# Two memory key tiles multiplied at the block border instead of in the first attention of block 2

## What is computed

```
memn = layer_norm_2(mem, ln_mem_g, ln_mem_b)          # once
def memory_cross_attn(x, memn, wq, wkv, wo):          # in each of the two layers of block 2
    q = x @ wq
    k, v = jnp.split(memn @ wkv, 2, axis=-1)          # does not depend on x
    ...
# border of the blocks
x = first_block(...)                                  # ends with layer_norm(x + ffn)
x = layer_norm_2(x, ln_in_g, ln_in_b)                 # second_block begins
h = x @ w_in[0]
```

## Time and profile before

| | us |
|---|---|
| median of 3 runs | 1728.51 |
| lowest and highest of them | 1723.71, 1728.75 |
| the profiled execution, its own time | 1727.46 |
| its span in the profile | 1725.7 |
| PE busy | 1577.0 (91%) |
| DVE busy | 1080.4 (63%) |
| ACT busy | 743.3 (43%) |

### The profile page before, as it was taken

How to read it: one execution, slowest core, us unless ns; L and a number is a source line. 1 busy time by engine, 2 the same in 40 slices (tenths; PEclk the granted TensorE clock), 3 DMA queues, 4 the chain that set the end, 5 groups by cost and what they waited for, 6 DMA issues and landing times.

```text
span 1725.7 us, 27579 instructions
## 1 busy us (share of the span) xinstructions
PE 1577.0 (91%) x11573; PEld 1491.7 (86%) x11573; DVE 1080.4 (63%) x1690; ACT 743.3 (43%) x1056; POOL 62.7 (4%) x58
## 2 busy tenths in 40 slices
PE   6889899999888999977989889999889899899996
PEld 6889899998788999967978888999889788889996
DVE  6975955556866864565444637767754546476766
ACT  4554433333463433332555344445435553344442
POOL 0200000000100000000000000000000000000000
PEclk8989999998899999997979999999988899999999
DMA  9423555554333565552522624655535146255551
GB/s 309 150 79 106 183 188 180 194 178 154 110 101 117 196 219 181 186 195 81 165 79 89 219 78 158 205 196 178 188 95 180 49 138 195 88 181 177 190 190 55
DMA packets 215423, 267.47 MB, mean 155 GB/s; under 512 B 7382, under 2 KB 196740, under 8 KB 215172
## 3 DMA queue, kind: packets, MB, share of 16 engines
q1 hardware_dynamic: 210404, 260.48, 46.1%
q10 hardware_dynamic: 4896, 5.25, 0.9%
HBM read 260.46 MB, written 5.24 MB: 154 GB/s over the span
## 4 chain that ended last, share of the span: by engine, by line
PE 76%; DVE 12%; DVEq 3%; ACT 3%; issue 2%; POOL 2%; DMA 0%; SPq 0%; POOLq 0%; ACTq 0%
PE psw L591 17%; PE psw L592 17%; PE psw L593 17%; PE psa L591 6%; PE psa L592 5%; PE psa L593 5%; DVE wlo L1336 3%; PE psa L727 2%; POOL rstd L1926 2%; PE psw L710 1%; PE psw L954 1%; DVE sy L1410 1%; DVE xtok L1365 1%; PE psw L1043 1%; PE psw L1025 1%
## 5 line engine op out<-in xcount | busy, mean ns | idle before, releaser
L1336 DVE TENSOR_TENSOR wlo<-raw,whi 128x2048 fp32r<-128x2048 f32 x226 | 511.1, 2265 | 328.0 <-ACT whi L1062 327.5
L1062 ACT ACTIVATE whi<-raw 128x2048 fp32r<-128x2048 f32 x226 | 427.0, 1889 | 364.0 <-PE psw L593 261.1
L591 PE MATMUL psw<-xhi,whi 128*128 128x256 f32 x1536 | 436.8, 284 | 2.6 <-ACT r L1195 1.4
L592 PE MATMUL psw<-xlo,whi 128*128 128x256 f32 x1536 | 436.1, 284 | 0.0
L593 PE MATMUL psw<-xhi,wlo 128*128 128x256 f32 x1536 | 435.8, 284 | 0.0
L591 PEld LDWEIGHTS psw<-xhi,whi 128*128 128x128 f32 x1536 | 296.3, 193 | 5.8 <-issue 2.8
L592 PEld LDWEIGHTS psw<-xlo,whi 128*128 128x128 f32 x1536 | 296.4, 193 | 1.2
L591 PE MATMUL psw<-whi,xhi 128*128 128x256 f32 (+2 forms) x992 | 289.4, 292 | 8.2 <-DVE xlo L1377 8.2
L593 PEld LDWEIGHTS psw<-xhi,wlo 128*128 128x128 f32 x1536 | 296.3, 193 | 0.0
L592 PE MATMUL psw<-wlo,xhi 128*128 128x256 f32 (+2 forms) x992 | 287.2, 290 | 0.0
L593 PE MATMUL psw<-whi,xlo 128*128 128x256 f32 (+2 forms) x992 | 286.8, 289 | 0.0
(11 more groups left out here) (249 smaller groups left out, 1964.6 us busy)
## 6 DMA issues: line engine op xcount, KB each, us to landing
raw<-in_w_gu SPq DMA_DIRECT2D x44, 1024.0 KB, 5.1
raw<-in_ffn_w_up SPq DMA_DIRECT2D x44, 1024.0 KB, 5.1
raw<-in_w_in SPq DMA_DIRECT2D x26, 1024.0 KB, 5.3
raw<-in_w_down SPq DMA_DIRECT2D x22, 1024.0 KB, 4.9
raw<-in_ffn_w_down SPq DMA_DIRECT2D x22, 1024.0 KB, 4.8
raw<-in_xa_wkv SPq DMA_DIRECT2D x16, 1024.0 KB, 5.4
raw<-in_w_o SPq DMA_DIRECT2D x8, 1024.0 KB, 5.0
raw<-in_w_pg SPq DMA_DIRECT2D x8, 1024.0 KB, 5.0
```

The costliest lines, as they stand in the source:

```text
L591: pe.matmul(o, lh, rh, start=first, stop=False)
L592: pe.matmul(o, lh, rl, start=False, stop=False)
L1062: nc.scalar.activation(tile_flat(whi, NW, i), tile_flat(raw, NL, i), ACT.Copy).then_inc(hi_ready, 1)
L1336: v.tensor_tensor(tile_flat(wlo, NL, i), tile_flat(raw, NL, i), tile_flat(whi, NW, i).bitcast(F32), ALU.subtract).then_inc(lo_ready, 1)
```

## The change

Tiles 0 and 1 of the memory keys of layer 1 of block 2 (`AT_BORDER`) leave the first attention stage of block 2 and stand in the order of tiles directly behind block 1's last tile. PE multiplies them there in four halves, each into a PSUM bank of its own (`psw`, banks 0 to 3), before `norm_turns`; ACT stores them there. The first attention stage of block 2 keeps four halves, in steps 2, 6, 10 and 12; steps 0, 4, 8 and 11 lose theirs. DVE's `serve` behind block 1's last tile moves to between the two token tiles of the norm, and two serves for the moved tiles follow behind the norm.

```diff
+SLOTS2_FIRST = (2, 6, 10, 12)
...
-    return [(block - 1, 4 * l + k) for k in range(4)]
+    return [(block - 1, 4 * l + k) for k in range(4)][2 if (block, l) == (2, 0) else 0:]
+AT_BORDER = [(1, 0), (1, 1)]
...
+    for lm, k in AT_BORDER:
+        tiles.append(((2, "kv", lm, k), rows(w["xa_wkv_2"][lm])[:, :, k * TC:(k + 1) * TC]))
...
     def memory_slot(block, l, step):
+        if (block, l) == (2, 0):
+            return 20 + SLOTS2_FIRST.index(step) if step in SLOTS2_FIRST else None
...
-                if n:
+                if n and not 16 < n < 20:
                     pe.wait_ge(kv_staged, n)
...
+            for n in range(16, 20):
+                memory_half(n, psw[:, n - 16, :])
+            pe.wait_ge(kv_staged, 20)
             norm_turns((2, "in", 0), psw)
...
+            for n in range(16, 20):
+                memory_store(n, stage[0][:, n % 2, :], psw[:, n - 16, :])
+                if n % 2:
+                    serve((2, "kv", 1, n // 2 % 8))
             for stored_half in kv_stored:
-                act.wait_ge(stored_half, 16 * 8)
+                act.wait_ge(stored_half, 16 * 10)
...
                     if next_key is not None:
                         norm(next_key, xtok, 2, lambda t: (dve.drain(), half_stats(xtok, t)), [t])
+                        if t == 0:
+                            serve(key)
...
-            serve((1, "d", L - 1, FS - 1))
+            serve((2, "kv", 1, 0))
+            serve((2, "kv", 1, 1))
```

More of the change, by code:

```diff
@@ L672, in p_turns, with memory_half @@
                 ins.then_inc(p_turned, 1)
-            def memory_half(n):
+            def memory_half(n, bank):
                 key, half = (2, "kv", n // 16, n // 2 % 8), n % 2
@@ L686, in memory_half @@
                     if key[3] < 4:
-                        ins = product(psa[:, 3, 0:TC], wh[:, k, piece], wl[:, k, piece], memhi[:, k, :],
+                        ins = product(bank[:, 0:TC], wh[:, k, piece], wl[:, k, piece], memhi[:, k, :],
                                       memlo[:, k, :], k == 0, k == KD - 1)
                     else:
-                        ins = product(psa[:, 3, 0:TC], memhi[:, k, piece], memlo[:, k, piece], wh[:, k, :],
+                        ins = product(bank[:, 0:TC], memhi[:, k, piece], memlo[:, k, piece], wh[:, k, :],
                                       wl[:, k, :], k == 0, k == KD - 1)
@@ L714, in attention @@
                     if n is not None:
-                        memory_half(n)
+                        memory_half(n, psa[:, 3, :])
                     if i - 2 >= first:
@@ L1079, in p_high, with memory_store @@
                 nc.scalar.activation(pT_hi, bank2(psw, bank), ACT.Copy).then_inc(p_hi, 1)
-            def memory_store(n, place):
+            def memory_store(n, place, bank):
                 if n % 2:
@@ L1088, in memory_store @@
                     act.wait_ge(kv_stored[n % 2], 16 * (n // 2))
-                nc.scalar.activation(place, psa[:, 3, 0:TC], ACT.Copy).then_inc(kv_staged, 1)
+                nc.scalar.activation(place, bank[:, 0:TC], ACT.Copy).then_inc(kv_staged, 1)
                 act.wait_ge(kv_staged, n + 1)
@@ L1114, in attention @@
                     if half is not None:
-                        memory_store(half, stage[block - 1][:, half % 2, :])
+                        memory_store(half, stage[block - 1][:, half % 2, :], psa[:, 3, :])
                     if i - 1 >= first:
```

## The result

The change made the kernel slower. The median went from 1727.92 us (6 runs of the kernel before, 1723.71 to 1728.75) to 1734.04 us (6 runs, 1732.32 to 1734.49); the ratio is 1.0038 with a 95% interval from 1.0026 to 1.0050, which is 4.5 to 8.6 us. The forecast was 1727.1, its range 1721.5 to 1733.0: the result lies outside.

The account below looks back on a forecast made before the run. PE was taken to carry 76% of the chain that ended last, DVE 12%, with the border DVE's and the attention PE's. Border +4.4 and attention -5.8 made -1.4 us, so 1727.1 from the median 1728.51; range 1721.5 to 1733.0.

Parts of the forecast that it names:

- Border, PE: nothing: Between blocks 1 and 2, the four moved halves fit PE's idle time, with 4.8 us of cover; no cost.
- Border, ACT and its DMAs: nothing: Between blocks 1 and 2, four stores and two more splits fit into ACT's idle time; no cost.
- Border, DVE: +4.4: Two more splits of 2.2 us ahead of `xlo` delay block 2's first product by 4.4 us, to about 795.3.
- Border, clock: 0: Before block 2's first product the clock falls again, with the same slow start behind it; no gain or loss.
- the clock holds over the border: Rival: halves keep PE working in the gap, the next product runs at full clock; -3.6 us, 1724.9, chance 0.10.
- Attention: -5.8: Block 2's first attention stage gains 5.8 us from losing the halves of steps 0, 4, 8 and 11.
- Step 0: First attention of block 2: without the half, PE's transposes start earlier; gain 0.8 us.
- Steps 11 and 12: First attention of block 2: `pv` no longer stands behind a half, the next waits for copies; gain 2.3 us.
- PEclk 1.00 throughout: Sign in block 2's first attention: PE's granted clock stays full while the stage takes 59.8 us.
- The clock falls in the attention: Rival: without halves, one stretch of some 14 us drops to 0.50; +7.2 us in sum, 1735.7, chance 0.06.
- PE bounds the attention wholly: Rival: all 11.2 us of PE work taken from the attention come back; -6.8 us in sum, 1721.7, chance 0.07.
- the halves were fully hidden: Rival: the attention gives back only steps 0 and 4, 1.3 us; +3.1 us in sum, 1731.6, chance 0.07.

Follow-up runs that it names:

- e2: Changed kernel with DVE's border splits reordered: one split before `xlo` as before the change, two behind it; 1729.50 us, ratio 1.0011 to the kernel before.
- e7: Changed kernel with 9 useless matmuls in each of steps 4 and 8 of the attention; attention 61.92 us, 1725.23 us in one run.
- e4: Changed kernel with its four remaining halves in steps 0, 4, 8 and 12 instead of 2, 6, 10 and 12; 1727.41 us, ratio 0.9987.
- e12: e5 unchanged, profiled a second time; attention 60.78 us with 4.3 at 0.50, 1720.09 us in one run.
- after: The changed kernel itself, in its first profile; attention 66.38 us with 17.5 at 0.50, median 1734.04 us, ratio 1.0038.
- e3: Kernel before with the four moved halves left out altogether, none at the border either; attention 72.96 us, 1734.79 us, ratio 1.0031.
- e10: Changed kernel, unchanged, profiled a second time; attention 66.36 us with 17.5 at 0.50, 1733.40 us in one run.
- e11: Changed kernel, unchanged, profiled a third time; attention 66.39 us with 17.5 at 0.50, 1733.09 us in one run.
- e5: Changed kernel with both the border order of e2 and the steps of e4; 1722.72 us, ratio 0.9976; its profiled attention 65.91 us with 15.5 at 0.50.
- e8: Changed kernel with the border order of e2 and 24 useless matmuls in each of steps 4 and 8; attention 61.99 us, 1724.82 us, ratio 0.9977.
- e6: Changed kernel with 24 useless matmuls in step 4 alone; attention 63.65 us, 1728.87 us in one run.
- e1: Changed kernel with 24 useless matmuls in each of steps 4 and 8 of the attention; attention 62.39 us, 1728.07 us, ratio 1.0001.

## Why the prediction was wrong

Step by step, in its own order.

- **Border, PE: nothing.** Right. The halves began 0.23 us behind the last matmul of block 1, where I had 0.4, and ended 4.86 us before the turns where DVE's order is the old one (e2); the cover had been put at 4.8.
- **Border, ACT and its DMAs: nothing.** Right: `xhi` was made as soon as the turns were, and e2, which keeps all stores, has the old border.
- **Border, DVE: +4.4.** Right: 29.31 - 24.90 = 4.41, and e2 takes all of it back. The place of the first product, 795.3, was not met (791.41), and nor was the range of 793 to 798 named for it, because this execution had reached the border 3.9 us earlier. I should have given it from PE's last matmul, not from the start of the span.
- **Border, clock: 0.** Right: the clock is at 0.50 from 778.5, when the halves have been over for 4.8 us, until 795.4, and the stage behind it took 92.10 us for 91.94. Filling the first half of the gap moved the fall and not the slow start. The rival "the clock holds over the border" fell with this. This also agrees with what the forecast cited from the Trainium skill (TensorE: Matmul & The Clock Gate, "HAM oscillation — how this bites in real kernels"), that behind a wait between bursts the next burst starts slow.
- **Attention: -5.8.** This is the step that failed; it came to +0.72. The terms were right at the clock for which they were worked out. Step 0: the transposes started 4.22 us behind the scores where it had been 5.02, the 0.8 forecast. Steps 11 and 12: from the half of step 10 to the end of the stage 17.72 us for 19.90, 2.2 us where 2.3 was forecast. Steps 4 to 12 together gave 5.03 of 5.0 in e7. What was named as a sign, no wait before `pv` in step 5, was seen (907.58 follows on 906.42), but because PE was slow and not because the copies were early. The whole stage took 60.6 and 60.8 us in e4 and e12, with 4 us at 0.50, against a forecast of 59.8 without any. What failed is the clause "PEclk 1.00 throughout", the clock's cost in the attention, which the sum had at nothing: PE was at half clock for 17.5 us, nearly all of them busy. By an estimate from these windows, the same work at full clock takes some 8.8 us less, and 66.38 - 59.8 = 6.6 of it reached the end of the stage; that the waits took in the rest is inferred. So the 0.8 us of step 0 was lost again at once, in transposes of 1.11 us and scores of 2.08.
- **The rivals.** "The clock falls in the attention", at 0.06, is what happened. Its size was near partly by luck: it let one stretch of 14 us fall, in steps 3 to 6 or 7 to 10, and got +8.6 for it; here two falls of 7 us and one of 3.5 cost 6.6, and the 3.5 came behind step 0, which it had not named. As a sum, +7.2 forecast by that rival stands against the measured +6.1, and 1735.7 against 1734.04. "PE bounds the attention wholly" and "the halves were fully hidden" are out by e7, e4 and e12: with the clock up, 5 us of the 11.2 come back, neither all nor the 1.3 of steps 0 and 4.
- **The range.** It was said to leave out what lies beyond -6 and +5 us, but 1721.5 to 1733.0 is -6.0 and +5.5 from the profiled execution and -7.0 and +4.5 from the median. The result lies outside by any of these.

**What misled me.** I took one stretch at 1.00, from 139.40 to 149.10 with PE busy for 6.85 us of 9.70, as evidence that pieces of this kind keep the clock, and gave the warning against it 0.06. Ahead of the fall at 901.0 PE was busy for 4.79 us of the 7.00, much the same share:

```profile
894.00:901.00 7.00, 4.79 (x43) 3.89 (x42) 4.30 (x22) 4.56 (x17) 0.00 (x0) 1.00 0.06 21
```

So the busy share of a stretch could not exclude a fall. The timeline of the stretch that I had leaned on, in the kernel before, shows what the share hides:

```profile
139.58 2.00 PE L727 MATMUL psa<-r,pt 128*128 128x64 f32 x16 [0.17 <-ACT pt L1124]
...
143.20 2.00 PE L727 MATMUL psa<-r,pt 128*128 128x64 f32 x16 [0.74 <-ACT pt L1124]
...
146.26 1.97 PE L648 MATMUL psw<-ident,r 128*128 128x128 f32 x16 [1.06 <-DVE r L1653]
```

Its idle comes in pieces of at most 1.06 us; ahead of the fall at 901.0 it is 2.32 in one piece, and PE was busy for 1.29 us of the last 3.50. That is a difference of the two stretches and no rule: e12 held the clock behind 1.79 us. I worked out that `pv` of step 4 would start only 0.5 us earlier than before. I did not write down what the same numbers say, that PE would be idle for 2.8 - 0.5 = 2.3 us there, which is just the wait measured, nor that it would be idle for 2.8 - 0.8 = 2.0 us in step 0, where 2.05 was measured. The section "A second HAM failure mode: psum-queue depth-cycling" of the same page of the Trainium skill tells of a kernel in which small idles between groups of matmuls made the clock swing; rows of after, e3, e10 and e11 agree with it in this stage (0.50 behind waits of 1.84 to 2.32 us), while those of e12 show a wait of 1.79 us without a fall.

**What is shown and what is open.** Shown: the border's 4.4 us are the two splits that were added ahead of `xlo` (e2). The attention's loss is the clock: more time at 0.50 went with a longer stage in after, e2 and e3 (17.5, 22.1 and 31.9 us with 66.4, 68.0 and 73.0) and in two executions of one kernel (e12 and e5), and matmuls that compute nothing shortened it (e8 against e2, e6 against after; e1 and e7 with the reservation above). The changed kernel repeats it (e10, e11). Open: why e4 and e12 mostly keep the clock with the same amount of work, and why the fall ends when it does. Their halves stand in every fourth step from 0, which is a matter of where the lumps of idle are and of when, but no run varied that alone: e4 and e5 also move a store on ACT and a split on DVE. That the waits bring the falls on is argued from what precedes them and from the fills, not shown for each: a wait of 1.79 us had a fall behind it in e5 and none in e4 and e12, and the wait of 1.84 us in step 8 had one in after and none in e6 for the next 6 us. Nor is it known how often e5_both falls; two profiles of it show two outcomes, and why executions enter the stage differently is open too. That the pieces of attention are narrow matmuls (64 to 256 columns) was not separated from their being thin in time. And whether any of the 3.4 us by which the rest differed (780.6 in all profiles of after, 777.2 and 780.8 in those of before) is the change's cannot be told from two profiles of before.

## What to carry to other kernels

Work that PE does "in a wait" may be what keeps the clock of TensorE up: before taking it away, list the idle that each removal uncovers, and price the work behind it at the half clock as well as at the full one. If filler has to move, leave what remains at the places with the longest waits (here steps 0, 4 and 8) rather than spread by convenience: e4 changed three numbers, and its ratio is 0.9987 where that of the changed kernel is 1.0038. It is no cure, since moving the halves opens other waits: in e4 and e12 the longest is now 3.74 us, in step 7, with the one fall behind it. And work moved into another engine's chain goes behind the operation that the next stage waits for: two splits moved behind `xlo` were worth 4.4 us, and both edits together made the version that beats the two kernels, 0.9976 (0.9959 to 0.9993) of the time before.

## What was not expected of the hardware

- Less work can take more time: e3 has about 11 us of PE's work less than the kernel before and a ratio of 1.0031 (1.0018 to 1.0043). About 2 us of useless matmuls (e7, twice 9 of them) went with a stage 4.5 us shorter than that of the changed kernel.
- In the changed kernel the falls of the clock repeated to the step in three executions: 887.5, 901.0 and 921.5 in after are 4.0, 17.5 and 38.0 us behind the scores of step 0, and in e10 and e11 they are 4.0, 17.5 and 38.0 too. In e5_both they did not repeat (15.5 and 4.3 us at 0.50).
- At 1.2 GHz a `pv` of 16 matmuls takes 3.67 us for 1.89, the eight transposes 1.91 for 1.05; scores of 128 columns only 1.23 for 0.71.
